# Two wide bfloat16 products ahead of each squaring in the recurrent stage of an RWKV-7 and sparse-attention decoder step

## The reference, cut to what matters

```python
def step(s, inp):
    r_t, w_t, k_t, v_t, kk_t, kka_t = inp
    s_kk = jnp.einsum('bhvk,bhk->bhv', s, kk_t)
    s = s * w_t[:, :, None, :] - s_kk[..., None] * kka_t[:, :, None, :] + v_t[..., None] * k_t[:, :, None, :]
    return s, jnp.einsum('bhvk,bhk->bhv', s, r_t)
```

## Time and profile before

| what | value |
| --- | --- |
| median of 3 runs | 3584.91 us (3572.67 to 3586.05) |
| profiled execution, its own time | 3590.75 us |
| its span, first to last instruction | 3588.7 us |
| TensorE busy | 3311.3 us (92% of the span) |
| VectorE / ScalarE / GpSimd busy | 2148.4 / 1096.0 / 488.6 us |
| mean granted TensorE clock | 0.92 of full speed |

### The profile page before, as it was taken

One profiled execution on the slowest core, in us unless ns is written; L12 is line 12 of the kernel. 1 busy time (PEld: TensorE's weight loads), 2 busy tenths in 40 slices (PEclk: granted clock), 3 DMA queues, 4 the chain that ended last, 5 costly groups with the idle time before them and its releaser, 6 DMA issues. The chain is left out here.

```text
span 3588.7 us, 73930 instructions
## 1 busy us (share of the span) xinstructions
PE 3311.3 (92%) x29593; PEld 1990.2 (55%) x29593; DVE 2148.4 (60%) x4302; ACT 1096.0 (31%) x2337; POOL 488.6 (14%) x687
## 2 busy tenths in 40 slices
PE   8999999999999999699998657888886899999998
PEld 4544445555555555366665436667765555555553
DVE  2028889999999999487765435565653344432211
ACT  4136650000000000255553126555552111111211
POOL 3330000000000000000000413343432100000000
PEclk9999999999999999799999877776665999999999
DMA  5241111111111111211000931221211511121110
GB/s 156 74 104 49 42 48 55 55 55 59 58 55 55 55 61 44 68 45 28 22 19 13 290 111 41 52 55 49 54 29 41 186 62 62 62 74 62 47 39 24
DMA packets 217448, 229.76 MB, mean 64 GB/s; under 512 B 28473, under 2 KB 195316, under 8 KB 216612
## 3 DMA queue, kind: packets, MB, share of 16 engines
q1 hardware_dynamic: 149624, 110.52, 11.4%
q0 software_dynamic: 21328, 52.96, 5.1%
q10 hardware_dynamic: 46172, 61.71, 5.0%
HBM read 156.58 MB, written 68.52 MB: 63 GB/s over the span
## 5 line engine op out<-in xcount | busy, mean ns | idle before, releaser
L409 PE MATMUL fro_acc<-h_t,fro_w 128*128 128x416 f32 x3280 | 1176.2, 516 | 0.0
L409 PEld LDWEIGHTS fro_acc<-h_t,fro_w 128*128 128x128 f32 x3280 | 615.3, 190 | 543.5 <-issue 536.6
L692 DVE TENSOR_SCALAR_CACHE_REDUCE fro_work<-scores,fro_real 128x384 uint8<-128x384 f32 (+6 forms) x462 | 656.2, 1474 | 2.1
L516 ACT ACTIVATE fro_out<-fro_acc 128x416 f32<-128x416 f32 (+3 forms) x230 | 118.0, 513 | 793.9 <-PE fro_acc L409 711.4
L2134 PE MATMUL mrg_po<-mrg_wo,mrg_mrg 128*128 128x512 f32 (+1 forms) x544 | 238.2, 596 | 4.5 <-DVE mrg_mrg L2239 4.5
L2970 DVE CUSTOM_DVE_ANT_0 att_seen<-att_ps,scores 128x512 f32<-128x512 f32 (+3 forms) x320 | 181.3, 607 | 97.1 <-PE att_ps L2856 96.9
L2166 PE MATMUL mrg_pg<-mrg_wg,mrg_x_t 128*128 128x512 f32 (+1 forms) x544 | 236.3, 592 | 0.0
L658 DVE SCALAR_TENSOR_TENSOR scores<-fro_work,w_idx,scores 128x512 f32<-128x512 f32 (+3 forms) x280 | 187.9, 671 | 40.1 <-ACT fro_work L573 13.2
L2134 PEld LDWEIGHTS mrg_po<-mrg_wo,mrg_mrg 128*128 128x128 f32 (+1 forms) x544 | 101.1, 186 | 138.7 <-issue 133.8
L2940 ACT ACTIVATE att_seen<-att_seen,att_shift 128x128 f32<-128x128 f32 (+15 forms) x128 | 152.6, 1194 | 81.0 <-DVE att_shift L2978 81.0
L573 ACT ACTIVATE fro_work<-fro_wk 128x512 f32<-128x512 f32 (+3 forms) x320 | 144.5, 540 | 92.5 <-PE fro_wk L482 91.6
(11 more groups left out here) (440 smaller groups left out, 4669.8 us busy)
## 6 DMA issues: line engine op xcount, KB each, us to landing
z_t<-fro_out ACTq DMA_DIRECT2D x180, 208.0 KB
fro_w<-in_w_in SPq DMA_DIRECT2D x41, 512.0 KB, 4.2
mrg_m_in<-z_t POOLq DMA_DIRECT2D x56, 256.0 KB, 3.4
sat_kv<-in_cache_kv SPq DMA_DIRECT2D x96, 128.0 KB, 3.4
sat_kv<-in_cache_kv POOLq DMA_DIRECT2D x96, 128.0 KB, 3.6
rwk_zi<-z_t SPq DMA_DIRECT2D x80, 129.0 KB, 2.7
z_t<-fro_out ACTq DMA_DIRECT2D x45, 192.0 KB
scores<-in_x_prompt SPq DMA_DIRECT2D x16, 512.0 KB, 8.3
```

The costliest lines, as they stand in the source:

```text
L409: last = pe.matmul(acc[e % 2][:, 0:CW], w[block_no % 3][:, kk, :], h_t[:, kk, CW * g:CW * g + CW], start=(kk == 0), stop=(kk == KD - 1))
L692: chain.mark(dve.tensor_scalar(junk[b % 2][:, 0:n], scores[:, c:c + n], realf[:, b:b + 1], None, op, ALU.add, accum_out=count[:, b:b + 1]))
```

## The change

Behind the waits of each squaring, and before its own products, `square` issues two products of the 128 by 128 bfloat16 identity `k.identb` with 512 columns of the bfloat16 constant `k.causal`. Each fills all 128 rows and 512 columns of `zz[:, 0, :]`, with `start=True`; the squaring then writes its own columns there, and only those are read. There are 80 squarings, so 160 such products. No semaphore, buffer or other instruction is added.

```diff
@@ def square(m, r), on TensorE
                 low = lower(gram[m % 2])
+                for _ in range(2):
+                    pe.matmul(zz[:, 0, :], k.identb[:, :], k.causal[:, 0:512], start=True, stop=True)
                 for b in range(BLK):
                     for p in range(4):
                         w = rows(p)
```

## The result

The change made the kernel slower by about half a per cent: a median of 3595.25 us (3591.05 to 3610.39, 7 runs) against 3577.79 us of the kernel before (3571.07 to 3588.28, 7 runs), a ratio of 1.0048 with a 95% interval of 1.0025 to 1.0070. I had forecast 15 us less. The profiled execution of the changed kernel took 3595.25 us, with a span of 3593.3 us.

The account below looks back on a forecast made before the run. VectorE and ScalarE bound a round's first part (unchanged, 18.6 us), TensorE the second: 16.0 + 0.9 = 16.9 us against 17.94, 1.04 us less over 15 rounds, so 15 us less: 3576 us profiled, range 3542 to 3607.

Parts of the forecast that it names:

- first part: Round from `grams` to `open_chunk` 2: set by VectorE's `centre_y` and ScalarE's list, to stay at 18.6 us.
- second part: Round from `open_chunk` 2 to the next `grams`: TensorE the bound, 16.9 us forecast against 17.94.
- the price of a pair: Two wide products ahead of a squaring on TensorE: 0.5 us at full level, 0.95 us at half.
- the direction of the clock: Recurrent stage: denser TensorE work raises the clock, full level beginning at squaring 1 or 2 and holding for the second part.
- I put both at 0: First part: pairs of squarings 0 and 1 hidden by waits before `turn_keys` and `open_chunk` 2; uncovered, up to 1.9 us a round.
- A mean near 0.95, thus about 16.0 us of base: Second part: full level holds, giving 16.0 us before the pairs' cost, between 15.74 at 1.00 and 16.27 at 0.87.
- 0.9 us a round on the path: Second part: pairs of squarings 2, 3 and 4 take 1.5 us at full level, 0.6 us of it absorbed by waits.
- D: Rival: pairs cost more than their cover, delaying `turn_keys`, `open_chunk` 2 and ScalarE's list; 3606 or 3650 us; chance 0.16.
- C: Rival: clock stays where it is, only the pairs' price is left; 16 us more, 3601 us; chance 0.20.
- B: Rival: whole round gets warm, first part as at 0.90, 16.69 us; 42 us less, 3543 us; chance 0.22.
- the sign for the price: Pair's records at L1339 should take 0.21 to 0.25 us each at full level; 0.44 or two a product means D.

Follow-up runs that it names:

- early_pairs: Two wide products only before squarings 0 and 1, against the kernel before the change: ratio 0.9991 (0.9975 to 1.0007).
- fill_and_all: The whole change plus two wide products in the wait ahead of `open_chunk` 2, against the kernel before the change: ratio 1.0021 (1.0000 to 1.0042).
- fill_and_late: Two wide products ahead of `open_chunk` 2 and pairs before squarings 2, 3 and 4, against the kernel before the change: ratio 0.9967 (0.9949 to 0.9984).
- the fill: Two wide products ahead of `open_chunk` 2, to the other bank of `zz`, none before squarings, against the kernel before the change: ratio 0.9974 (0.9956 to 0.9992).
- late_pairs: Two wide products only before squarings 2, 3 and 4, against the kernel before the change: ratio 1.0049 (1.0024 to 1.0075).

## Why the prediction was wrong

Its reading of the profile held in the main: a first part bound by VectorE and ScalarE, a second part bound by TensorE while the clock is low. So did the price of a pair (0.5 and 0.95 us forecast, 0.53 and 0.96 measured), and the direction of the clock. The forecast sum was 29 us of clock gain (1.94 x 15) less 13.5 us for the late pairs (0.9 x 15). Measured by the table's bookkeeping it was some 20 us of gain against a price of 37. By the profile a first part came to 19.77 us instead of 18.6 and a second part to 17.75 us instead of 16.9. Three steps failed.

"I put both at 0", for squarings 0 and 1. The cover was read off the idle time ahead of `turn_keys` and `open_chunk` 2, but the first thing behind squaring 0's pair is `solve` 1, and VectorE's copy of it stands ahead of the row sums on which ScalarE's list hangs. In the kernel before, that copy starts at most 12.45 us behind `grams`, and other work keeps the part at up to 19.68 us anyway, which hid this; with the pair ahead of it, it starts at 13.37 us or later in seven rounds, and the part grows with it. First parts grew by 1.17 us a round (16.4 us over 14). The pair of squaring 0 is 0.97 us of it in each of those seven rounds; the rest, a late `solve` 0 among it, is not explained, and first parts grew by 0.65 us a round with late pairs alone. By experiments the early pairs' price is 12 us (early_pairs) to 19 us (fill_and_all less fill_and_late). That they alone don't make the kernel slower is, by the bookkeeping, because the clock pays them back (0.934 against 0.925).

"A mean near 0.95, thus about 16.0 us of base". The second parts reached 0.84 in the profile, up from 0.76. The full level did begin early, and then in 4 of 14 rounds was gone again about the wait ahead of `open_chunk` 2, so that the part ran at 0.67; three more also began at the half level and came to 0.81 to 0.85. That this place matters is shown by the fill: with it in that wait the second parts come to 0.90 and 16.74 us with no pair at all.

"0.9 us a round on the path", for the late pairs, was right only as a mean of two unlike cases. At the full level their price is 0 (15.74 us with three pairs and with none: VectorE's copy of `solve` 3 starts 8.90 us into the part in both profiles, and its list runs from there to the next `grams` without a break, which is a likely bound, though no run took it apart). At 0.65 to 0.67 it is 1.7 us (19.24 to 20.93 us). The change has both kinds of round, and late_pairs prices them at 18 us in all.

Of the rivals, D had the right sign and part of the mechanism, ScalarE's list running late, but by another way than it named: not by a pair dearer than its cover, since the price was as forecast. C was wrong about the clock; that its 16 us over come so near to the 17 us measured is luck. B took its first part of 16.69 us from the last round of the loop, where ScalarE has 24 instructions instead of 31 or 32. With ScalarE's full work a first part took 18.36 us in the changed kernel at a clock of 1.00 throughout, and one 17.06 us in the kernel before at 0.86: the clock alone doesn't set it. And the sign for the price, records of 0.21 to 0.25 us at L1339, was badly chosen: the shortest of the 160 records is 0.376 us, since each lasts beyond the start of the next; the price is the distance from start to start.

What stays open: why squarings 3 and 4 together bring the mean clock below that of the kernel before (0.918), while each alone raises it (0.928 and 0.927) and the fill under them raises it to 0.9345. Why `solve` 0 comes late in some cold rounds, and why first parts grow with late pairs alone, is open too. Perhaps which rounds begin cold depends on all lengths before; the runs show the effect and not its rule. Nor is the price column more than a straight line through executions.

## What to carry to other kernels

Work added only to keep TensorE's clock up belongs where TensorE waits and its result goes to a bank that nobody waits for; ahead of a product that others wait for, it is paid at the half level in just those stretches that it was meant to heal. To know whether an insertion is covered, follow what is queued behind it on its own engine to the first consumer on another one, in rounds of every kind, and not only to the next idle time. And where the clock takes part, single edits need not add up: time them together.

## What the runs showed of the hardware that was not expected

Products of equal column count and number, with nearly equal time on TensorE (62.1 and 71.1 us), left mean clocks of 0.936 and 0.9065: those over 128 rows and 128 columns of the array raised the share of the full level, those over 32 by 32 lowered it, and in the gap the two kinds left 0.931 and 0.921. The Trainium skill, page "TensorE: Matmul & The Clock Gate", section "What's actually happening", has the gate follow how busy TensorE has been recently; here the products that kept TensorE occupied the longer left the lower clock, so in these kernels it also mattered what a product fills.

One VectorE instruction, `centre_y`, took between 0.68 and 4.76 us in the 16 times it runs in the kernel before, with one shape. In the round of the earlier trace rows GpSimd was working beside it, and it ended 0.55 us behind this one of GpSimd's:

```profile
2451.35 1.46 POOL L1157 TENSOR_TENSOR rwk_pm<-rwk_zi,param 128x768 f32<-128x768 f32 x1
```

The same 0.55 us stand in the changed kernel's round at 2296.18 us, where `centre_y` took 2.92 us. So the 4.29 us that the prediction read as its length look like a wait for GpSimd; no run moves GpSimd's work to show it.

The same program varies by 36 us between executions (3567.03 to 3602.70 us for the kernel before), and the mean granted clock goes with it, at 1.65 us for 0.001 on the straight line (correlation -0.82 in 148 executions).
